# Neighbourhood attention of sample and prompt as one item on one TensorE schedule

## What is computed

```python
def row_step(args):
    i, q_row = args
    rs = jnp.clip(i - kh // 2, 0, rows - kh)
    k_r = lax.dynamic_slice_in_dim(k, rs, kh, axis=1)[:, :, colidx_j]
    v_r = lax.dynamic_slice_in_dim(v, rs, kh, axis=1)[:, :, colidx_j]
    ...
    s = jnp.einsum('bnqhd,bmnkhd->bhnqmk', qb, k_r).astype(jnp.float32) * scale + bias + col_mask
    p = jax.nn.softmax(s.reshape(bsz, NA_HEADS, nqb, NA_QB, kh * NA_KB), axis=-1).reshape(s.shape)
    o = jnp.einsum('bhnqmk,bmnkhd->bnqhd', p.astype(v.dtype), v_r)
    return o.reshape(bsz, GRID_W, NA_WIDTH)
```

## Time and profile before

| what | us |
|---|---|
| median of 3 runs (1384.11 to 1387.12) | 1386.08 |
| span of the profiled execution | 1375.9 |
| TensorE busy in it | 1178.5 |
| z projection with attention, first scores to block 7 | 186.09 to 315.90 |
| z projection, rest of it, to the last z transposes | 315.90 to 427.9 |
| first expert weights asked for by SP | 732.49 |

### The profile page before, as it was taken

How to read it: one execution, slowest core, us unless ns; L and a number is a source line. 1 busy time by engine, 2 the same in 40 slices (tenths; PEclk the granted TensorE clock), 3 DMA queues, 4 the chain that set the end, 5 groups by cost and what they waited for, 6 DMA issues and landing times.

```text
span 1375.9 us, 29721 instructions
## 1 busy us (share of the span) xinstructions
PE 1178.5 (86%) x13063; PEld 727.2 (53%) x13063; DVE 421.8 (31%) x742; ACT 348.6 (25%) x749; POOL 280.7 (20%) x254
## 2 busy tenths in 40 slices
PE   5899999999997898988899958997788878888765
PEld 3555555555454787877755535554444444444432
DVE  2100043434565555666437361000000000000017
ACT  3200024353323554565532111110010010010003
POOL 0100012221326343367412001111111111111000
PEclk9999999999997899999999978999999999999987
DMA  9894231122435211221407169999999999999966
GB/s 319 325 337 164 69 94 62 54 82 72 153 123 141 68 39 38 50 57 27 172 7 310 70 262 327 398 390 397 401 404 405 408 404 404 398 395 396 411 270 249
DMA packets 82025, 314.74 MB, mean 229 GB/s; under 512 B 13808, under 2 KB 28488, under 8 KB 65150
## 3 DMA queue, kind: packets, MB, share of 16 engines
q1 hardware_dynamic: 75862, 298.96, 58.5%
...
q10 hardware_dynamic: 936, 1.61, 0.3%
...
## 4 chain that ended last, share of the span: by engine, by line
PE 28%; DMA 27%; DVE 5%; ACT 4%; issue 3%; SPq 1%; POOL 0%; DVEq 0%; POOLq 0%; ACTq 0%
DMA arena<-in_exp_w 26%; PE bank L1585 10%; PE bank L2472 6%; PE bank L1855 6%; PE bank L2490 2%; PE bank L1609 2%; SPq L2326 1%; DVE arena L1466 1%; PE bank L2211 1%; PE bank L2459 1%; DMA arena<-pick_out 1%; DVE arena L1453 1%; DVE arena L2577 0%; ACT arena L1295 0%; DVE arena L1483 0%
## 5 line engine op out<-in xcount | busy, mean ns | idle before, releaser
L2472 PE MATMUL bank<-arena 128*64 128x256 f32 x2048 | 256.8, 409 | 67.9 <-DMA arena<-in_exp_w 58.1
L907 PE MATMUL bank<-arena 128*128 128x512 f32 (+1 forms) x736 | 256.3, 497 | 4.4 <-POOL arena L493 1.6
L2472 PEld LDWEIGHTS bank<-arena 128*64 128x64 f32 x2048 | 158.7, 147 | 175.4 <-DMA arena<-in_exp_w 70.0
L1585 PE MATMUL bank<-arena 64*64 64x64 f16 (+3 forms) x7184 | 204.7, 221 | 36.4 <-issue 12.6
L1585 PEld LDWEIGHTS bank<-arena 64*64 64x64 f32 (+2 forms) x7184 | 183.2, 127 | 63.6 <-issue 35.9
L907 PEld LDWEIGHTS bank<-arena 128*128 128x128 f32 x736 | 133.9, 189 | 99.4 <-issue 85.0
L2490 PE MATMUL bank<-arena 128*64 128x512 f32 x512 | 118.6, 605 | 17.5 <-ACT arena L2416 17.5
L2438 DVE TENSOR_TENSOR arena<-bank,arena 128x256 f32<-128x256 f32 x32 | 13.6, 424 | 303.5 <-PE bank L2472 303.5
L2363 POOL DMA_INDIRECT arena<-h_scratch,arena x32 | 30.8, 962 | 362.5 <-PE bank L2459 260.7
L1855 PE MATMUL bank<-arena 128*128 128x512 f32 x192 | 86.4, 597 | 0.0
L2490 PEld LDWEIGHTS bank<-arena 128*64 128x64 f32 x512 | 34.8, 137 | 79.3 <-issue 55.7
...
## 6 DMA issues: line engine op xcount, KB each, us to landing
arena<-in_exp_w SPq DMA_DIRECT2D x96, 2048.0 KB, 44.7
...
```

The lines of the kernel that those rows point to most:

```text
L907: return nc.tensor.matmul(bank[i % 3][:, 0:GR[p] * GW], w[:, k, :], hT[:, k, PART[p]], start=(k == 0), stop=(k == KD - 1))
L1585: return nc.tensor.matmul(out, lhsT, r, start=start, stop=True, skip_group_check=True)
L2472: ins = nc.tensor.matmul(bank[b + 2 * c.s][BLK * n:BLK * n + BLK, 0:HALF], xT[c.s][:, j, :], slot[c.w][:, j, n * HALF:(n + 1) * HALF], sta ...
```

## The change

Sample and prompt of a block of columns and a pair of heads become one item, so there are 16 items in place of 32, with three slots in a block, after `k` = 0 and 5 of the long half and `k` = 2 of the short one. In a slot, TensorE first turns the probabilities of item `q-2` and then computes the scores of item `q`, four products. The value product of `q-2` moves out of the slot to `slot_end`, two or three projection steps later (`k` = 2 and 7 of the long half, `k` = 5 of the short one). The prompt's scores go to columns of bank 4 behind the sample's, its turned probabilities and its output to columns of bank 7. ScalarE copies the turned probabilities first, then takes the exponentials of `q`, then copies the output. VectorE does two additions and two maxima for an item and one reciprocal for both. GpSimd divides both parts under one signal. The division of item `q` still stands behind the scores of `q+1` on VectorE. In SP's queue the fourth band moves ahead of the slab `weights(9)`. The buffers for scores stay three deep for sample and for prompt.

```diff
@@ -307,12 +307,11 @@
             return 6 + (i - 3) // 2, (i - 3) % 2
 
 
-        items = [(g, n, hp) for n in range(NQB) for hp in range(NPAIR) for g in range(2)]
+        items = [(n, hp) for n in range(NQB) for hp in range(NPAIR)]
         assert len(items) == NI
         KIND = [0, 1, 1, 2]
-        SLOTS = {0: 0, 2: 1, 5: 2, 7: 3}
-        PER = 5
-        TB, RB = 2, 3
+        PER = 3
+        TB = 2
...
@@ -398,14 +397,14 @@
             band_load(1)
             weights(6)
             weights(7)
-            sp.wait_ge(sem("s_added"), 8)
+            sp.wait_ge(sem("s_added"), 4)
             bias_load(2)
             weights(8)
+            sp.wait_ge(sem("o_mm"), 4)
+            band_load(2)
             sp.wait_ge(sem("o_mm"), 8)
-            band_load(2)
+            band_load(3)
             weights(9)
-            sp.wait_ge(sem("o_mm"), 16)
-            band_load(3)
             sp.wait_ge(sem("s_added"), NI)
             for d in range(2):
                 half = slice(d * 64, d * 64 + 64)
...
@@ -442,16 +441,12 @@
                 pool.wait_ge(sem("col_ready"), 2 * (k // 4 + 1))
                 modulated(nc.gpsimd.tensor_scalar, k, 1).then_inc(sem("h_pool"), 1)
 
-            for j, (g, n, hp) in enumerate(items):
+            for j in range(NI):
 
                 pool.wait_ge(sem("p_inv"), j + 1)
-                if g == 0:
-                    p = sc_s[(j // 2) % 3]
-                    ins = nc.gpsimd.tensor_tensor(p, p, pinv[:, j, :].unsqueeze(2).to_broadcast([P, 2, 8 * KB]), ALU.mult)
-                else:
-                    p = sc_p[(j // 2) % 3]
-                    ins = nc.gpsimd.tensor_scalar(p, p, pinv[:, j, 0:1], None, ALU.mult)
-                ins.then_inc(sem("p_ready"), 1)
+                s3, p = sc_s[j % 3], sc_p[j % 3]
+                nc.gpsimd.tensor_tensor(s3, s3, pinv[:, j, 0:2].unsqueeze(2).to_broadcast([P, 2, 8 * KB]), ALU.mult)
+                nc.gpsimd.tensor_scalar(p, p, pinv[:, j, 2:3], None, ALU.mult).then_inc(sem("p_ready"), 1)
 
...
@@ -599,30 +594,24 @@
 
             def slot(q):
 
+                j = q - TB
+                if 0 <= j < NI:
+                    act.wait_ge(sem("pT_mm"), j + 1)
+                    nc.scalar.copy(pT_s[j % 2], bank[6])
+                    nc.scalar.copy(pT_p, bank[7][:, 2 * P:3 * P]).then_inc(sem("pT_ready"), 1)
                 if q < NI:
-                    g = items[q][0]
                     act.wait_ge(sem("s_max"), q + 1)
-                    for e in range(2 - g):
-                        p = sc_p[(q // 2) % 3] if g else sc_s[(q // 2) % 3][:, e, :]
+                    for e in range(3):
+                        p = sc_p[q % 3] if e == 2 else sc_s[q % 3][:, e, :]
                         ins = nc.scalar.activation(p, p, ACT.Exp, bias=nmax[:, q, e:e + 1], accum_out=psum_row[:, q, e:e + 1])
                     ins.then_inc(sem("p_exp"), 1)
-                j = q - TB
                 if 0 <= j < NI:
-                    g = items[j][0]
-                    act.wait_ge(sem("pT_mm"), j + 1)
-                    if j >= 2 + 2 * (1 - g):
-                        act.wait_ge(sem("o_mm"), j - 1 if g else j - 3)
-                    if g:
-                        ins = nc.scalar.copy(pT_p[0], bank[6][:, 0:P])
-                    else:
-                        ins = nc.scalar.copy(pT_s[(j // 2) % 2], bank[6])
-                    ins.then_inc(sem("pT_ready"), 1)
-                j = q - RB
-                if 0 <= j < NI:
-                    g, n, hp = items[j]
+                    n, hp = items[j]
                     act.wait_ge(sem("o_mm"), j + 1)
-                    nc.scalar.copy(grid(catT[:, hp, :], g, n * QB, QB),
-                                   bank[7][:, 0:GR[g] * QB].rearrange("p (r c) -> p r c", c=QB)).then_inc(sem("o_ready"), 1)
+                    for g in range(2):
+                        ins = nc.scalar.copy(grid(catT[:, hp, :], g, n * QB, QB),
+                                             bank[7][:, P * g:P * g + GR[g] * QB].rearrange("p (r c) -> p r c", c=QB))
+                    ins.then_inc(sem("o_ready"), 1)
...
@@ -757,26 +744,22 @@
             def slot(q):
 
                 if q < NI:
-                    g, n, hp = items[q]
+                    n, hp = items[q]
+                    s3, p = sc_s[q % 3], sc_p[q % 3]
                     dve.wait_ge(sem("s_mm"), q + 1)
-                    if q >= 6:
-                        dve.wait_ge(sem("pT_mm"), q - 5)
-                    if g:
-                        p = sc_p[(q // 2) % 3]
-                        nc.vector.tensor_tensor(p, bank[4][:, 0:4 * KB], bias_p[:, KIND[n], hp, :], ALU.add).then_inc(sem("s_added"), 1)
-                        dve.wait_ge(sem("s_added"), q + 1)
-                        nc.vector.tensor_reduce(nmax[:, q, 0:1], p, AX, ALU.max, negate=True).then_inc(sem("s_max"), 1)
-                    else:
-                        p = sc_s[(q // 2) % 3]
-                        nc.vector.tensor_tensor(p, pair_banks(4, 8 * KB), bias[:, KIND[n] % 2, 2 * hp:2 * hp + 2, :], ALU.add).then_inc(sem("s_added"), 1)
-                        dve.wait_ge(sem("s_added"), q + 1)
-                        nc.vector.tensor_reduce(nmax[:, q, :], p, AX, ALU.max, negate=True).then_inc(sem("s_max"), 1)
+                    if q >= 3:
+                        dve.wait_ge(sem("pT_mm"), q - 2)
+                    own.done(nc.vector.tensor_tensor(s3, pair_banks(4, 8 * KB), bias[:, KIND[n] % 2, 2 * hp:2 * hp + 2, :], ALU.add))
+                    nc.vector.tensor_tensor(p, bank[4][:, 8 * KB:12 * KB], bias_p[:, KIND[n], hp, :], ALU.add).then_inc(sem("s_added"), 1)
+                    own.wait(own.n)
+                    nc.vector.tensor_reduce(nmax[:, q, 0:2], s3, AX, ALU.max, negate=True)
+                    dve.wait_ge(sem("s_added"), q + 1)
+                    nc.vector.tensor_reduce(nmax[:, q, 2:3], p, AX, ALU.max, negate=True).then_inc(sem("s_max"), 1)
                 j = q - 1
                 if 0 <= j < NI:
                     dve.wait_ge(sem("p_exp"), j + 1)
-                    e = 2 - items[j][0]
-                    nc.vector.reciprocal(pinv[:, j, 0:e], psum_row[:, j, 0:e]).then_inc(sem("p_inv"), 1)
-                if q == 18:
+                    nc.vector.reciprocal(pinv[:, j, 0:3], psum_row[:, j, 0:3]).then_inc(sem("p_inv"), 1)
+                if q == 9:
                     dve.wait_ge(sem("bias_in0"), 32)
...
@@ -963,55 +944,55 @@
 
             def scores(q):
 
-                g, n, hp = items[q]
-                nq, nk = GR[g] * QB, GR[g] * KB
+                n, hp = items[q]
                 pe.wait_ge(sem("s_added"), q)
-                at = TOFF[g] + n * nq
+                for g in range(2):
+                    nq, nk = GR[g] * QB, GR[g] * KB
+                    at = TOFF[g] + n * nq
+                    for e in range(2):
+                        rows = slice(64 * e, 64 * e + 64)
+                        out = bank[4][64 * e:64 * e + 64, 8 * KB:8 * KB + nk] if g else bank[4 + e][:, 0:nk]
+                        ins = nc.tensor.matmul(out, qT[rows, hp, at:at + nq], grid(kT[rows, hp, :], g, band(n), KB), start=True, stop=True)
+                ins.then_inc(sem("s_mm"), 1)
+
+            def probs_turned(j):
+
+                pe.wait_ge(sem("p_ready"), j + 1)
+                pe.wait_ge(sem("o_ready"), j)
                 for e in range(2):
-                    rows = slice(64 * e, 64 * e + 64)
-                    out = bank[4][64 * e:64 * e + 64, 0:nk] if g else bank[4 + e][:, 0:nk]
-                    ins = nc.tensor.matmul(out, qT[rows, hp, at:at + nq], grid(kT[rows, hp, :], g, band(n), KB), start=True, stop=True)
-                ins.then_inc(sem("s_mm"), 1)
-
-            def probs_turned(j):
-
-                g = items[j][0]
-                pe.wait_ge(sem("p_ready"), j + 1)
-                pe.wait_ge(sem("pT_ready"), j)
-                if g:
-                    ins = nc.tensor.transpose(bank[6][:, 0:P], sc_p[(j // 2) % 3], ident)
-                else:
-                    for e in range(2):
-                        for s in range(2):
-                            at = (2 * e + s) * P
-                            ins = nc.tensor.transpose(bank[6][:, at:at + P], sc_s[(j // 2) % 3][:, e, s * P:(s + 1) * P], ident)
-                ins.then_inc(sem("pT_mm"), 1)
+                    for s in range(2):
+                        at = (2 * e + s) * P
+                        nc.tensor.transpose(bank[6][:, at:at + P], sc_s[j % 3][:, e, s * P:(s + 1) * P], ident)
+                nc.tensor.transpose(bank[7][:, 2 * P:3 * P], sc_p[j % 3], ident).then_inc(sem("pT_mm"), 1)
 
             def values(j):
 
-                g, n, hp = items[j]
+                n, hp = items[j]
                 pe.wait_ge(sem("pT_ready"), j + 1)
-                pe.wait_ge(sem("o_ready"), j)
                 pe.wait_ge(sem(f"band_in{n % 2}"), 16 * 12 * (n // 2 + 1))
-                for s in range(2 - g):
-                    for e in range(2):
```

(38 more changed lines are left out.)

18 lines of the change are left out of this document (7 added, 11 removed).

## The result

| | median us | runs | ratio to before, 95% interval |
|---|---|---|---|
| before | 1385.09 (1382.69 to 1387.12) | 4 | |
| changed | 1366.15 (1364.02 to 1371.47) | 4 | 0.9869 [0.9847, 0.9891] |

The change is faster by 18.9 us. Of the 9.0 us between forecast and time, 1.0 is the kernel before, whose median of four runs is 1385.09, where the forecast started from 1386.08 for three.

What follows compares the result with a forecast made beforehand. TensorE was taken to set the pace. Attention of 43.2 + 0.5 + 0.6 + 0.4 = 44.7 us against 55.6 saves 10.9, so span 1375.9 becomes 1365.0; with 10.2 on top, 1375.2 us, range 1371 to 1382.5.

Steps and rivals of the forecast that it cites:

- What bounds the stage: In the z projection with attention, TensorE sets the pace; a microsecond it saves or waits moves everything behind it.
- The pieces: TensorE's work for a merged item: slot 1.75 and end of slot 0.95, 2.70 us, times 16 = 43.2.
- joined value product: On TensorE, values of sample 0.59 and prompt 0.26 us, less one change of shape, 0.09, since they touch.
- The waits: TensorE's 5.0 us of waits go; new ones for the division: 0.6 us at the third slot, 0.4 at item 8.
- The chain: From a slot's first transpose through scores, maximum and division: 5.4 us, fitting with 0.3 us to spare in seven short intervals.
- rival 1: The chain from slot to slot is 0.8 us longer than its rows: gain 7, time 1379 us; chance 0.16.
- rival 4: GpSimd's division is held by VectorE on the way to every slot: 4 us slower, 1390; chance 0.06.
- Rival 2: On TensorE, fewer changes of tile shape save nothing and only waits go: 4.5 us, time 1381.6; chance 0.07.
- SP's queue: Loads of the bands, the slab of weights and the gate weights, in their new order, cost nothing.
- The stage in sum: Attention takes 44.7 us after the change against 55.6 before, 10.9 us less.
- rival 3: Behind the stage, a longer stretch of low granted TensorE clock gives the gain back: time 1386 us; chance 0.07.
- work around the span: The median of the runs stands 10.2 us above the profiled span; this part was taken as unchanged.

Runs made afterwards that it cites:

- values_split: The changed kernel with the prompt's value product one projection step behind the sample's; 1370.72 us (one run).
- after_hole64: The changed kernel with 64 satisfied waits (32 instructions) added on TensorE at the idle end of stage 1; 1374.37 us, ratio 0.9937.
- after_third: The changed kernel unchanged, run again beside the kernels with added waits; 1367.59 us, ratio 0.9891.
- after_waits64: The changed kernel with 64 more waits (32 instructions) at the start of TensorE's queue; 1372.38 us, ratio 0.9896.

## Why the prediction was wrong

**What bounds the stage: right.** TensorE still goes from piece to piece; in the stretch it is busy 117.05 of 117.53 us.

**The pieces: right in kind, 0.06 too much each.** An item was put at 2.70 and takes 2.64, so 16 of them 42.2 instead of 43.2. The term that was mis-sized is the joined value product, 0.70 instead of 0.76; values_split shows why: joining saves 0.16, not 0.09. The slot is 1.64 and 0.10 on the way back, 1.74 instead of 1.75. With 0.20 for the interruption, the end of the slot is 0.90, 0.95 forecast. The rule of the Trainium skill (TensorEngine Tiling (Array Packing), Key Properties) that a change of tiling mode drains TensorE agrees in kind with these rows; it names no size.

**The waits: right.** The first transposes wait 0.36 (0.6 expected). At item 8 the mask runs into the division, as forecast: VectorE's mask and GpSimd's division of the changed kernel are

```profile
244.96 2.26 DVE L717 TENSOR_TENSOR arena<-arena 128x2048 f32<-128x2048 f32 x1
```

```profile
245.13 2.99 POOL L448 TENSOR_TENSOR arena<-arena 128x512 f32<-128x512 f32 x1 [4.04 <-DVE arena L761]
248.10 0.60 POOL L449 TENSOR_SCALAR arena<-arena 128x128 f32<-128x128 f32 x1
```

The division takes 2.99 instead of the 1.04 of the other items, and TensorE's three steps ahead of the transposes 2.97 instead of 2.68: 0.3 us (0.4 expected), where the one wait in rows 2 was 2.2.

**The chain: right.** In the interval that starts at 217.57, from the slot's first transpose to the end of the division is 5.2 us, 5.4 expected, against 5.67 from slot to slot:

```profile
221.17 1.04 POOL L448 TENSOR_TENSOR arena<-arena 128x512 f32<-128x512 f32 x1 [4.04 <-DVE arena L761]
222.19 0.60 POOL L449 TENSOR_SCALAR arena<-arena 128x128 f32<-128x128 f32 x1
```

So rival 1 (a longer chain) and rival 4 (the division held in every slot) fell: the division took 1.04 and 0.60 in each item but one. Rival 2 (changes of shape save nothing) fell with the 2.64. SP's queue cost nothing, as costed.

**The stage in sum: 1.4 too little.** The attention takes 43.3 (117.5 less the 74.2 of projection and z transposes): 42.2 for the items, 0.36 and 0.29 for the two waits, 0.4 in small gaps, against 44.7 forecast. 12.3 us gained instead of 10.9.

**The step that failed: all gain was looked for in the stage.** The sum held that everything behind it only moves along ("a microsecond that it saves or waits moves everything behind it"), and had no term for the recurrence. The one rival that looked there, rival 3, expected a loss by the clock. In its place the runs showed a gain: 18.9 us less the 12.3 of the stage leave 6.6 behind it, and the recurrence was shorter in each profiled execution of the changed kernel (251.2, 252.1 and 251.7 us) than in either of before (257.0 and 261.4). Two things lie in that. One is the place of TensorE's stops for instructions, which the 32 wait instructions saved by the merging shift: put back to the old places, they cost 6.4 us in the median (after_hole64 against after_third). The other is the clock, rival 3 with the opposite sign: from 423 to 469 us, the same part of the work as rows 10, it was 0.84 against the 0.79 there, and over the recurrence 0.98 against 0.95. In the first pair of executions this is all of the 5.8 us. Why the clock was higher isn't known, and how much of the 6.6 in the medians each of the two makes stays open.

That 12.3 and 6.4 add up to 18.7 is in part luck, since they come from different series. With the stops put back, the gain is 8.1 us in one series (before 1382.47, after_hole64 1374.37, where the change itself gained 14.9) and 13.6 in another (before 1385.96, after_waits64 1372.38), on either side of the forecast 10.9.

**A second mistake, which hid the scatter.** The 10.2 us between span and median were called work around the span. By the estimate above they are 1.8 us of that and 8.4 by which this one execution was shorter than the median. As the gain was taken off the median, the number didn't suffer, but the reading did: the executions of before differ by 4 us at the first scores and by 4.4 in the recurrence, and the range of 1371 to 1382.5 was made of cases of the stage alone and left no room for that. Span to span, the forecast 1365.0 became 1362.3: 1.4 from the stage and 5.8 from the recurrence less, 3.0 more because this execution came later to its first scores (189.09 against 186.09), and 1.5 more in the later parts.

**What stays open.** The share of clock and stops in the gain behind the stage, as said. Why the stops cost more at one place than at another isn't read from a row; the stop at record 6988 was 0.7 us in one execution of before and 2.1 in the other. And which part of the 1.5 us given back behind the recurrence is scatter wasn't tried.
